# Dropping the zero-state products of the first prompt tile, and moving the delta rule's first scores between the levels of its inverse

## The reference

```
# mLSTM (retention has the same shape, without m and n)
num = w_inter * (q @ c) + (q @ k.T * exp(dmat - m)) @ v
den = w_inter * (q @ n) + sum(s)
c   = dec * c + (k * wk).T @ v          # c0 = n0 = 0 for the prompt
# gated delta rule; tri = 1 + strictly lower (beta k k^T gam)
u = solve(tri, v * beta);  w = solve(tri, k * beta * eg)
v_new = u - w @ s
o     = (q * eg) @ s + ((q @ k.T) * gam) @ v_new
s     = exp(g_last) * s + (k * exp(g_last - G)).T @ v_new   # s0 = 0 for the prompt
```

## Time and profile before

| what | value |
|---|---|
| time, median of 3 runs (lowest to highest) | 1509.55 us (1509.17 to 1512.14) |
| span of the profiled execution | 1507.5 us |
| PE, DVE, ACT busy | 1317.3, 476.7, 246.9 us |
| first mixer | start to about 260 us |
| experts of layer 0 | about 260 to 715 us |
| second mixer, of it the first prompt tile | about 715 to 1035 us, of it about 846 to 937 us |
| experts of layer 1 | about 1035 to 1500 us |

### The profile page before, as it was taken

The page is one execution under the profiler, slowest core; times in us unless marked ns, Lnnn a source line. Parts: engine busy times, 40 slices in busy tenths (PEclk is TensorE's granted clock), DMA queues, the critical chain, the costliest instruction groups (busy, mean ns, idle before and its releaser), DMA issues.

```text
span 1507.5 us, 35631 instructions
## 1 busy us (share of the span) xinstructions
PE 1317.3 (87%) x15774; PEld 850.6 (56%) x15774; DVE 476.7 (32%) x1244; ACT 246.9 (16%) x632; POOL 64.4 (4%) x100
## 2 busy tenths in 40 slices
PE   8999889999897887887899978988999888798795
PEld 6655546555554554554478666556566455455453
DVE  1033445432132121221344746344222222122132
ACT  2122213111000100010322412223001001000011
POOL 2000003000000000000200100010000000000000
PEclk8999799999999999999899989999999999999998
DMA  9743135999999999999634200137999999999996
GB/s 298 143 93 113 70 119 216 376 401 427 429 428 429 427 430 428 428 429 420 176 113 138 88 4 15 45 143 316 395 403 427 430 427 430 428 428 429 427 430 254
DMA packets 53002, 454.01 MB, mean 301 GB/s; under 512 B 5552, under 2 KB 6096, under 8 KB 28352
## 3 DMA queue, kind: packets, MB, share of 16 engines
q1 hardware_dynamic: 51024, 448.35, 73.6%
q0 software_dynamic: 1904, 4.58, 1.1%
HBM read 449.55 MB, written 3.35 MB: 300 GB/s over the span
## 4 chain that ended last, share of the span: by engine, by line
PE 70%; DMA 19%; DVE 6%; issue 3%; ACT 1%; POOL 0%; DVEq 0%; SPq 0%; ACTq 0%; POOLq 0%
PE bank L325 68%; DMA W<-in_moe_w_up 18%; PE bank L328 2%; DVE zT L2149 1%; DVE zT L2144 1%; DMA conv_sb<-in_conv_state 1%; DVE zT L2154 1%; DVE HN L1449 1%; DVE HN L1469 0%; DMA X<-in_x_prompt 0%; DVE TM L1449 0%; DVE X L1449 0%; DVE W L1449 0%; DVE gain L1449 0%; DVE W L1469 0%
## 5 line engine op out<-in xcount | busy, mean ns | idle before, releaser
L325 PE MATMUL bank<-W,zT 128*32 128x128 f32 (+2 forms) x10304 | 661.1, 404 | 85.1 <-DMA W<-in_moe_w_gate 32.0
L325 PEld LDWEIGHTS bank<-W,zT 128*32 128x32 f32 (+1 forms) x10304 | 387.5, 125 | 324.7 <-DMA W<-in_moe_w_gate 42.8
L2144 DVE TENSOR_TENSOR zT<-zT,bank 128x128 f32<-128x128 f32 x64 | 18.4, 288 | 464.5 <-PE bank L325 464.5
L325 PE MATMUL bank<-W,HT 128*32 128x128 f32 (+1 forms) x768 | 136.1, 390 | 5.7 <-issue 2.6
L325 PE MATMUL bank<-HT,W 128*128 128x288 f32 x512 | 128.9, 412 | 3.1 <-ACT zT L1179 3.1
L1422 ACT COPY zT<-bank 32x256 f32<-32x256 f32 x128 | 46.7, 364 | 448.9 <-PE bank L325 447.3
L325 PEld LDWEIGHTS bank<-HT,W 128*128 128x128 f32 x512 | 97.3, 192 | 31.0 <-ACT zT L1179 3.8
L325 PE MATMUL bank<-zT,HN 128*128 128x128 f32 (+1 forms) x832 | 103.0, 283 | 1.0 <-DVE HN L1449 0.7
L325 PEld LDWEIGHTS bank<-zT,HN 128*128 128x128 f32 (+1 forms) x832 | 97.4, 195 | 8.8 <-issue 7.4
L2154 DVE COPY zT<-bank 32x256 f32<-32x256 f32 x128 | 53.3, 416 | 137.2 <-PE bank L325 135.2
L325 PEld LDWEIGHTS bank<-W,HT 128*32 128x32 f32 (+1 forms) x768 | 61.2, 139 | 59.5 <-issue 54.5
(11 more groups left out here) (276 smaller groups left out, 918.2 us busy)
## 6 DMA issues: line engine op xcount, KB each, us to landing
W<-in_moe_w_down SPq DMA_DIRECT2D x64, 2048.0 KB, 23.2
W<-in_moe_w_gate SPq DMA_DIRECT2D x62, 2048.0 KB, 21.3
W<-in_moe_w_up SPq DMA_DIRECT2D x62, 2048.0 KB, 22.6
W<-in_ab_w_in SPq DMA_DIRECT2D x8, 2048.0 KB, 14.6
W<-in_c_w_in SPq DMA_DIRECT2D x8, 2048.0 KB, 17.3
W<-in_ab_w_out SPq DMA_DIRECT2D x2, 2048.0 KB, 7.8
TM<-in_moe_w_gate SPq DMA_DIRECT2D x2, 2048.0 KB, 20.0
zT<-in_moe_w_up SPq DMA_DIRECT2D x2, 2048.0 KB, 19.0
```

Of the source, the lines that this page charges most:

```text
L325: return nc.tensor.matmul(out, lhsT, rhs, start=start, stop=stop)
L2144: v.tensor_tensor(hid[u % 2], sg[u % 2], banks[u % 2][:, 0:P], ALU.mult).then_inc(m["hidden"], 1)
```

## The change

In tile 0 of the first mixer, `half` no longer multiplies q by the state or by n; DVE writes the outputs and the states straight from the banks instead of adding to them; the clearing of the state is gone. In tile 0 of the second mixer `half` is no longer called. The values are scaled by beta when they are first copied to tokens: by DVE in one product for four heads, by ACT in four operations, one for each head, instead of one copy. The scores q·k of both halves, their turning and the scaled keys are worked between the levels of the inverse, in place of products of constants there. Behind the inverse stand new values, outputs and states of both halves without the state's products, with the sample's steps between them in another order and fewer products of constants.

```diff
@@ half() on PE
-                bank = L0.open(pe)
-                for h in range(4):
-                    last = mm(bank[:n, h * P:h * P + P], q(h), st[:, 4 * f + h, :])
-                L0.close(last)
-                if mlstm:
+                if t:
+                    bank = L0.open(pe)
+                    for h in range(4):
+                        last = mm(bank[:n, h * P:h * P + P], q(h), st[:, 4 * f + h, :])
+                    L0.close(last)
+                if t and mlstm:
...
+            def first_values():
+                E["r_ready"].wait(pe)
+                E["tm_act"].wait(pe)
+                for f in range(2):
+                    bank = L1.open(pe)
+                    for h in range(4):
+                        last = mm(bank[:, h * P:h * P + P], UI[f][:, h, :], TM[:, 16 + 4 * f + h, :])
+                    L1.close(last)
+            def first_outputs(f):
+                E["vn_ready"].wait(pe)
+                E["st_ready"].wait(pe)
+                bank = L0.open(pe)
+                for h in range(4):
+                    last = mm(bank[:, h * P:h * P + P], first_ST[f][:, h, :], YI[f][:, h, :])
+                L0.close(last)
+                E["kw_ready"].wait(pe)
+                bank = L0.open(pe)
+                for h in range(4):
+                    last = mm(bank[:, h * P:h * P + P], first_kw[f][:, h, :], YI[f][:, h, :])
+                L0.close(last)
...
@@ the levels, PE
                         elif lv == 0:
                             sample_read_state()
-                        meanwhile(0 if t else 2, L1)
+                            meanwhile(2, L1)
+                        elif lv == 2:
+                            first_scores_T(0)
+                        else:
+                            first_scores(lv // 2)
                         block_level_t(t)
...
                     else:
-                        meanwhile(2, L1)
+                        first_scores_T(1)
                     pairs_y()
...
                     if not t:
-                        meanwhile(8, L1)
-                        sample_state()
                         meanwhile(4, L1)
                     for f in range(2):
                         E["tu_ready"].wait(pe)
...
+                    else:
+                        first_values()
+                        first_outputs(0)
+                        sample_state()
+                        first_outputs(1)
+                        sample_flip_y()
+                        S["yT"].wait(pe)
...
+                        output_sample(side)
...
                     else:
-                        meanwhile(16, L1)
+                        meanwhile(12, L1)
@@ ACT, tile's values to tokens
-                    do(nc.scalar.copy(TM[:n, 20:24, :], heads4(bank[:n, :])), L1.taken)
+                    if t:
+                        do(nc.scalar.copy(TM[:n, 20:24, :], heads4(bank[:n, :])), L1.taken)
+                    else:
+                        for h in range(4):
+                            do(nc.scalar.activation(TM[:, 20 + h, :], bank[:, h * P:h * P + P], ACT.Copy,
+                                                    scale=beta[:, 4 + h:5 + h]), L1.taken if h == 3 else None)
@@ DVE
-                        if not t and lv == 0:
-                            sample_read_state()
+                        if not t:
+                            (sample_read_state, lambda: first_scores(0), lambda: first_keys(0),
+                             lambda: first_scores(1))[lv]()
...
+                        sample_values_wide()
+                        for f in range(2):
+                            first_outputs(f)
+                        sample_scale_y()
                         sample_state()
+                        sample_y_T()
+                        add_output_sample(side)
```

More of the change, by code:

```diff
@@ L575, in half, with first_scores, first_scores_T @@
                     L0.close(last)
+            def first_scores(f):
+                bank = L0.open(pe)
+                for h in range(4):
+                    q, k = [zT[:, base + 4 * f + h, COL[0]:COL[0] + P] for base in (0, 8)]
+                    last = mm(bank[:, h * P:h * P + P], q, k)
+                L0.close(last)
+            def first_scores_T(f):
+                E["s_ready"].wait(pe)
+                bank = L1.open(pe)
+                for h in range(4):
+                    last = flip(bank[:, h * P:h * P + P], first_S[f][:, h, :], P)
+                L1.close(last)
[3 more added lines that the diff above has]
+                for f in range(2):
+                    bank = L1.open(pe)
+                    for h in range(4):
+                        last = mm(bank[:, h * P:h * P + P], UI[f][:, h, :], TM[:, 16 + 4 * f + h, :])
+                    L1.close(last)
+            def first_outputs(f):
[6 more added lines that the diff above has]
+                E["kw_ready"].wait(pe)
+                bank = L0.open(pe)
+                for h in range(4):
+                    last = mm(bank[:, h * P:h * P + P], first_kw[f][:, h, :], YI[f][:, h, :])
+                L0.close(last)
             def finish_half(t, f):
@@ L1211, in y_squares, with scores_T, new_values @@
                 square_sums(Yout[:n, 4 * f:4 * f + 4, :], scratch[:n], hss[:n, 4 * f:4 * f + 4], E["hss_act"], scale)
-            def scores_T(n):
+            def scores_T(n, dst=ST):
                 bank = L1.take(act)
-                do(nc.scalar.copy(ST[:n, :, :n], heads4(bank[:n, :])[:, :, :n]), L1.taken)
+                do(nc.scalar.copy(dst[:n, :, :n], heads4(bank[:n, :])[:, :, :n]), L1.taken)
                 E["st_ready"].mark(act.nop())
+            def new_values(n, f):
+                bank = L1.take(act)
+                do(nc.scalar.copy(YI[f][:n, :, :], heads4(bank[:n, :])), L1.taken)
+                E["vn_ready"].mark(act.nop())
             def layer_ab():
@@ L1361, in layer_c @@
                             squares(x, ws[:, 0:1024])
+                    if t == 0:
+                        for f in range(2):
+                            new_values(n, f)
                     for f in range(2):
-                        if t == 1 and f:
-                            take_gates(t, 7)
-                        scores_T(n)
-                        bank = L1.take(act)
-                        do(nc.scalar.copy(YI[f][:n, :, :], heads4(bank[:n, :])), L1.taken)
-                        E["vn_ready"].mark(act.nop())
+                        if t:
+                            if f:
+                                take_gates(t, 7)
+                            scores_T(n)
+                            new_values(n, f)
                         y_squares(n, f, GAM[f], float(P) ** -0.5)
@@ L1568, in half @@
                     between()
[L1569 to L1570 removed]
+                if t:
+                    bank = L0.take(dve)
+                    tt(tmp[:n], heads4(bank[:n, :]), bc_last(wq, P), ALU.mult, L0.taken)
                 if mlstm:
                     red(den[:n, :], Sm[:n, :, :n])
[L1573 to L1575 removed]
+                    if t:
+                        bank = L0.take(dve)
+                        tt(den2[:n, :], bank[:n, 0:4], wq, ALU.mult, L0.taken)
+                        tt(den[:n, :], den[:n, :], den2[:n, :], ALU.add)
                     ts(den2[:n, :], den[:n, :], -1.0)
@@ L1871, in layer_c @@
                         signal(E["tu_ready"])
-                    if not t:
-                        sample_state()
-                    signal(E["state_ready"])
-                    for f in range(2):
-                        o = lambda w: c_out[:, t, w + 4 * f:w + 4 * f + 4]
-                        half(t, f, GAM[f][:n, :, :n], o(0), o(8), o(16), 8 + 4 * f, 16 + 4 * f, delta=o(24),
-                             between=first_norm if t and f else None)
-                        if not t:
-                            (sample_flip_y, lambda: add_output_sample(side))[f]()
+                    if t:
+                        signal(E["state_ready"])
+                        for f in range(2):
+                            o = lambda w: c_out[:, t, w + 4 * f:w + 4 * f + 4]
+                            half(t, f, GAM[f][:n, :, :n], o(0), o(8), o(16), 8 + 4 * f, 16 + 4 * f, delta=o(24),
+                                 between=first_norm if f else None)
+                    else:
+                        sample_values_wide()
+                        for f in range(2):
+                            first_outputs(f)
+                        sample_scale_y()
+                        sample_state()
+                        sample_y_T()
+                        add_output_sample(side)
                     signal(E["state_done"])
```

86 lines of the change are left out of this document (54 added, 32 removed).

## The result

The changed kernel took 1496.43 us in the median of four runs (1493.22 to 1499.96), the kernel before beside it 1509.36 (1507.41 to 1512.14): a ratio of 0.9912, interval 0.9892 to 0.9932. The forecast was 1501.0, its range 1497.0 to 1504.5: the sign was right, and the gain of 12.9 was half as large again as the 8.6 forecast. The profiled execution of the changed kernel was the longest of its four, 1499.96 with a span of 1498.1, so that the two profiles differ by 9.4 only. Its mean granted clock is also the lowest of the four, 0.969 where the shortest run has 0.973.

The account below looks back on a forecast made before the run. PE bounds the kernel, its mixers being chains where a microsecond saved counts in full. Terms -1.5 - 0.5 + 1.1 + 0.5 - 10.2 + 2.0 = -8.6 bring the span 1507.5 to 1498.9; plus 2.05, forecast 1501.0, range 1497.0 to 1504.5.

Parts of the forecast that it names:

- First mixer, forecast -2.0: Tile 0 without products with the zero state: -1.5 in the mLSTM, -0.5 in the retention.
- If the clock rises at the same moment, the earlier start is spent partly at half rate: Retention, tile 0: outputs start 0.7 earlier, but only 0.35 is won in this case; -0.5 taken.
- ACT's copies, +1.1: Second mixer, ahead of the inverse: one copy becomes four scaled operations, unhidden, lengthening PE's wait from 1.34 to about 2.4.
- Inserts, +0.5: Scores and scaled keys between the inverse's levels nearly fit the gaps; bounds nothing to +2.8.
- Tail, -10.2 + 2.0 = -8.2: From the inverse's end to the addition to X: reordered work saves 10.2; a half-slow output product costs 2.0.
- The rule weighed there: Tail's output product: idle PE starts the next group cold, so the whole product is slow; by it alone 1502.7.
- Behind the addition, 0: Everything after DVE's addition to X stays as it was, even with twelve fillers for sixteen.
- the experts' loops would be as long as before: Both experts' loops keep their length, so their starts move by 2 and by 8.6.
- waited out at the experts: Rival: the second layer's first experts wait for weights, so the second mixer's 6.6 is lost; about 1507.5, chance 0.06.
- the low clock does not end: Rival: half rate outlasts the thinner tail, costing 9.1 or more; from 1510 on, chance 0.04.
- the clock holds: Rival: no clock fall in the tail's idle, so the 2.0 is not paid; 1497 to 1499, chance 0.20.

Follow-up runs that it names:

- before: The kernel without the change, unedited; 1509.36 us in the median beside the changed kernel.
- after: The changed kernel as first measured and profiled, against the kernel before; 1496.43 us, ratio 0.9912.
- after_again: The changed kernel once more, unedited, for more runs and a second profile; 1495.15 us, 0.9934 of the kernel before.
- second_only: Changed kernel with only the second mixer's part; the first mixer's tile 0 multiplies by the cleared state again; 1494.60 us, 0.9919 of the kernel before.
- after_16: Changed kernel with sixteen products of constants, as before, in place of twelve ahead of the turn of tile 0's outputs; 1495.47 us, 0.9924 of the kernel before.
- first_only: Kernel before with only the first mixer's part of the change, second mixer as before; 1509.36 us, 1.0021 of the kernel before.
- one_copy: Changed kernel with ACT's single plain copy in place of four scaled ones, that beta scaling left out; 1495.78 us, 0.9917 of the kernel before.
- Tail_filled: Changed kernel with ten and four products of constants added around the sample's turn, in PE's idle stretches of the tail; 1497.12 us, 0.9933 of the kernel before.
- The delays: Changed kernel with 14, 24 or 34 products of constants in place of 4 behind tile 0's inverse; 1502.75, 1508.83, 1500.77 us, one run each.
- delay_24: Changed kernel with 24 products of constants in place of 4 behind the inverse, ahead of the new values; 1508.83 us, one run.
- delay_34: Changed kernel with 34 products of constants in place of 4 behind the inverse, ahead of the new values; 1500.77 us, one run.
- no_inserts: Changed kernel with scores, their turning and scaled keys moved behind the inverse, products of constants again between its levels; 1498.41 us, 0.9939 of the kernel before.

## Why the prediction was right or wrong

It named the changed steps and most of their sizes, and missed what the clock would do behind them. Against the two profiles of before stand four of the new second mixer (after, after_again, second_only, after_16; for the first mixer those three that have its change):

- **First mixer, forecast -2.0; 0.0 in the stage.** The mechanism was right: from the first scores to the product for n it is 7.72 in all twelve profiles with the change and 9.33 in the five without, -1.6, and the retention's outputs 0.8 earlier in the profiled pair. The sum failed at "If the clock rises at the same moment, the earlier start is spent partly at half rate": the low stretch there did not stay put but got longer (3.78 for 2.50), and another behind it took the rest. The other profiles of the changed first mixer range from 166.05 to 172.06, those of the old one from 168.75 to 176.87; over all seventeen the means are 170.2 and 171.5, so -1.3. First_only's times show no gain.
- **ACT's copies, +1.1; +1.0 in the lead.** Right, and PE's wait of 2.33 is the 2.4 named. What follows that wait was missed: the clock falls at the first level, which one_copy takes away.
- **Inserts, +0.5; the inverse +1.3** in the mean of the four (35.6 against 34.3). Mis-sized, inside its bounds; of the +2.5 in the first profile a part is chance. The 1.3 is not the inserts' alone: taking out either them (34.06) or ACT's three operations with the low stretch behind them (34.16) brings the inverse back to before's length.
- **Tail, -10.2 + 2.0 = -8.2; -9.2** (20.1 against 29.3), and -8.1 in the profiled pair. Right in mechanism and close in size: behind the idle of 2.83 the clock falls, and a part of the output product runs slow: it takes 5.03 to 6.30 in the four profiles, for 3.66, so +1.4 to +2.6. Tail_filled prices that at 2.5. The rule weighed there, from the Trainium skill, "TensorE: Matmul & The Clock Gate", section "HAM oscillation — how this bites in real kernels", that PE left idle between groups starts the next one cold, agrees with this place. The time that the prediction drew from it, the whole product slow, does not: 6.30 at most in the four, where twice the full rate's time would be 7.3.
- **Behind the addition, 0; -4.6** (tile 1 with the routing 106.3 against 110.9). This is the step that failed: "Behind the addition all stays as it was". The work did stay as it was; its clock did not. With the tail 9 us shorter and the inverse other, the dip in tile 1 is no longer answered by a low stretch, and the next one falls into PE's wait ahead of the routing instead of into the routing. The five profiles with the second mixer as before, edits of it included, take 109.7 to 117.7 for the two stages, those four 105.6 to 107.4. The 4.6 itself is an estimate: both profiles of before are of executions longer than its medians in the later comparisons (1506.1 to 1508.2). The delays speak for the moment of the dip as the cause, so it could not be read from the rows of before, and it is no lasting gain of the new order: with ten products of constants more, 3.3 of the 4.6 are gone, with twenty more all of it, with thirty 2.2.

Together 0.0 + 1.0 + 1.3 - 9.2 - 4.6 = -11.5, where the medians say -12.9 and -11.1, and the ratios of the four comparisons with the new second mixer (0.9912 to 0.9934) 10 to 13. Start-up, unedited, moved by up to 3.4 us between profiles. The forecast that the experts' loops would be as long as before was right for the second: from the first group of 256 columns to the end 452.5 and 452.4. Of the rivals, "waited out at the experts" and "the low clock does not end" are both out; "the clock holds" gave the nearest time, 1497 to 1499, for a wrong reason.

What exactly decides whether a given dip is answered stays open. The Trainium skill, "TensorE: Matmul & The Clock Gate", section "What's actually happening", says that the point at which the clock changes varies from run to run of one kernel. The runs of one kernel here scatter by 3.5 to 21 us, which fits; the two profiles each of before and of after agree on whether the dip in tile 1 is answered and on the stretch at the routing, which does not speak for pure chance.

Within one kernel the time follows the mean granted clock: first_only took 1498.46 at 0.977 and 1519.39 at 0.963. Between the two orders it does not: the eight runs of after_again average 0.970 and the 19 of before beside them 0.973, and the changed kernel is still the shorter by 11.1. So the new order does not have less low clock. That more of it lies where PE waits anyway is what the profiles show at the routing; for the runs that were not profiled it is not shown.

## What to carry to other kernels

In a chain of small products, price a change by stages, and give every later stage in which PE dips a term of its own: here low stretches that moved in unedited code were worth some 4.6 us of 11.5, by two profiles against four. An idle of a few microseconds costs its length and, where PE sets the pace behind it, what the low clock takes: 1.0 more of waiting for ACT brought a low stretch that a plain copy did not. And fillers that keep the clock up are worth only what the next dip leaves of them: in the one profile of it, filling the tail won 2.5 there and lost 3.0 in the next tile.

## What the runs showed of the hardware

- The same dip (1.76 of 3.00 busy in before and in delay_24, 1.75 in delay_34) was followed by a granted clock of 0.61, 0.70 and 1.00.
- PE's idle of 2.33 to 2.34 ahead of the inverse was followed by half rate in ten profiles of ten, an idle of 1.34 to 1.42 in none of seven.
- One engine's single copy of 128x512 (0.58) made into four scaled ones took 1.57, and moved the next table load and PE's wait by the same 1.0; POOL's doing the scaling instead brought the lead back to 17.15.
- Runs of one kernel scattered by 3.5 to 21 us, and the longer ones had the lower mean granted clock (first_only 0.977 to 0.963, before beside after_16 1500.24 at 0.977 and 1511.05 at 0.969). Between kernels the mean clock does not order the times: delay_34 and no_inserts have 0.973 and 0.974 with spans of 1498.9 and 1495.6, after_again 0.969 with 1496.3.
